# A scan step with re-paired and padded matmuls, another VectorE order, square sums on GpSimd, and the two layers written out

## The reference, cut to what matters

```
for l in range(DEPTH):
    f = swiglu(rmsnorm(x, ffn1_pre)); x = x + 0.5 * rmsnorm(f, ffn1_post)
    m, ssm, conv, pool = mixer(rmsnorm(x, mix_pre)); x = x + rmsnorm(m, mix_post)
    f = swiglu(rmsnorm(x, ffn2_pre)); x = x + 0.5 * rmsnorm(f, ffn2_post)

# the scan inside the mixer, per head, in chunks of 128 tokens
xbc = silu(conv4(xbc))                                # xs, B, C
y_intra = (C Bt * L) @ (xs * dt)                      # L: decays inside a chunk
cs = Bt @ (xs * dt * decay_to_end)                    # state that a chunk adds
state = state * chunk_decay + cs                      # chained over the chunks
y = y_intra + (C @ state_before) * exp(acum) + d_skip * xs
y = rmsnorm(y * silu(z)) @ w_ssd_branch
```

## Time and profile before

| | |
|---|---|
| timed runs (median, 3) | 2205.31 us (2205.11 to 2212.32) |
| the profiled execution, whole | 2213.59 us |
| its span, first to last instruction | 2211.8 us |
| mean granted TensorE clock | 0.964 |
| PE busy | 2081.6 us, 94% of the span |
| DVE, ACT, POOL busy | 952.4, 932.1, 1245.7 us |

### The profile page before, as it was taken

One profiled execution on the slowest core, in us unless ns is written; L12 is line 12 of the kernel. 1 busy time (PEld: TensorE's weight loads), 2 busy tenths in 40 slices (PEclk: granted clock), 3 DMA queues, 4 the chain that ended last, 5 costly groups with the idle time before them and its releaser, 6 DMA issues.

```text
span 2211.8 us, 40913 instructions
## 1 busy us (share of the span) xinstructions
PE 2081.6 (94%) x13546; PEld 2023.1 (91%) x13546; DVE 952.4 (43%) x2010; ACT 932.1 (42%) x1357; POOL 1245.7 (56%) x555
## 2 busy tenths in 40 slices
PE   6999889999999998999879998899999999989997
PEld 6999888988899997999879998889898999989997
DVE  3221177676545535221142212767665454352212
ACT  4433345555333434333334333455553334444332
POOL 5666643434356665667656666433443666656665
PEclk9999989999899999999989999999997999999998
DMA  4445423444344443444424454234433444434443
GB/s 168 142 142 158 149 74 107 128 135 140 119 141 137 142 144 103 136 143 149 143 86 142 145 155 141 80 100 138 138 127 111 156 143 140 143 96 141 142 154 109
DMA packets 86339, 292.40 MB, mean 132 GB/s; under 512 B 15728, under 2 KB 15728, under 8 KB 86256
## 3 DMA queue, kind: packets, MB, share of 16 engines
q1 hardware_dynamic: 68544, 249.13, 36.2%
q10 hardware_dynamic: 17712, 42.22, 5.5%
HBM read 269.29 MB, written 22.02 MB: 132 GB/s over the span
## 4 chain that ended last, share of the span: by engine, by line
PE 83%; DVE 8%; DVEq 3%; issue 2%; POOL 1%; ACT 1%; DMA 1%; ACTq 0%; POOLq 0%; SPq 0%
PE gb L1015 25%; PE gb L1019 23%; PE gb L1018 23%; DVEq L700 2%; PE kb L1129 2%; PE kb L1151 1%; PE kb L1137 1%; DVE gb L746 1%; POOL wlo L354 1%; PE kb L1166 1%; PE gb L1067 1%; PE kb L1160 1%; PE kb L1112 1%; PE gb L1070 1%; PE gb L1071 1%
## 5 line engine op out<-in xcount | busy, mean ns | idle before, releaser
L354 POOL TENSOR_TENSOR wlo<-wraw,whi 128x1024 fp32r<-128x1024 f32 x474 | 1139.1, 2403 | 883.3 <-ACT whi L429 864.2
L1015 PE MATMUL gb<-ahi,whi 128*128 128x336 f32 x2256 | 751.0, 333 | 23.9 <-ACT bc L496 8.2
L1019 PE MATMUL gb<-ahi,wlo 128*128 128x336 f32 x2256 | 723.0, 320 | 0.0
L1018 PE MATMUL gb<-alo,whi 128*128 128x336 f32 x2256 | 722.3, 320 | 0.0
L429 ACT ACTIVATE whi<-wraw 128x1024 fp32r<-128x1024 f32 x474 | 494.8, 1052 | 187.2 <-PE gb L1015 116.7
L1015 PEld LDWEIGHTS gb<-ahi,whi 128*128 128x128 f32 x2256 | 432.7, 192 | 38.6 <-issue 19.9
L1018 PEld LDWEIGHTS gb<-alo,whi 128*128 128x128 f32 x2256 | 433.2, 192 | 0.0
L1019 PEld LDWEIGHTS gb<-ahi,wlo 128*128 128x128 f32 x2256 | 431.0, 191 | 0.0
L1015 PE MATMUL gb<-bhi,whi 128*128 128x336 f32 x1248 | 394.7, 316 | 5.1 <-DVE blo L969 5.1
L1018 PE MATMUL gb<-blo,whi 128*128 128x336 f32 x1248 | 392.7, 315 | 0.0
L1019 PE MATMUL gb<-bhi,wlo 128*128 128x336 f32 x1248 | 392.4, 314 | 0.0
(11 more groups left out here) (166 smaller groups left out, 2177.1 us busy)
## 6 DMA issues: line engine op xcount, KB each, us to landing
wraw<-wts SPq DMA_DIRECT2D x474, 512.0 KB, 3.5
ssm_o<-tail ACTq DMA_DIRECT2D x32, 576.0 KB, 3.2
st<-ssm_in ACTq DMA_DIRECT2D x32, 512.0 KB, 3.6
x<-x_in ACTq DMA_DIRECT2D x2, 672.0 KB, 4.9
y<-x ACTq DMA_DIRECT2D x2, 672.0 KB, 3.0
pool_o<-tail ACTq DMA_DIRECT2D x2, 540.0 KB, 4.9
tail<-pst_in ACTq DMA_DIRECT2D x2, 480.0 KB, 4.2
conv_o<-cso ACTq DMA_DIRECT2D x48, 13.5 KB, 3.2
```

Of the source, the lines that this page charges most:

```text
L354: pool.tensor_tensor(wlo[:, s, :], wraw[:, s, :], whi[:, s, :].bitcast(F32), ALU.subtract).then_inc(w_lo, 1)
L1015: ins = pe.matmul(gb[bank][:, 0:T], whi[:, slot, w], xh, start=first and j == 0, stop=False)
L1018: pe.matmul(gb[bank][:, 0:T], whi[:, slot, w], xl, start=False, stop=False)
L1019: ins = pe.matmul(gb[bank][:, 0:T], wlo[:, slot, w], xh, start=False, stop=last and j == tiles - 1)
```

## The change

Five parts.

1. **Matmul shapes.** `halfr` gets 128 rows (the lower 64 zero), so L1106 contracts over 128 rows. The first chunk-state product takes all 128 rows; `bcur`'s rows outside the meta tokens are zeroed once per layer, and `group_b` becomes two copies. The intra-chunk products go chunk by chunk with the two heads side by side. The sample update becomes eight products of 32 rows, alternately on rows 0 to 31 (bank `kb2`) and 32 to 63 (bank `kb3`). The zero product is made once per layer.
2. **PE's order.** The sample update and the transposes stand ahead of the inter-chunk products; a new semaphore `yi_full` tells when the intra products are there.
3. **DVE's order.** The taps of the convolution stand between the steps of the state chain; `d_skip * xs + y_intra` is one operation right behind the chain and gives `y_read`; the states' update stands ahead of y.
4. **Square sums.** POOL adds y's squares to `acc`, with the semaphore `y_sum` for ACT, POOL itself and the mean.
5. **Layers written out.** Python loops take the place of `Fori(0, DEPTH)` on every engine, and `update_x` at the end of layer 0 interleaves the first `split_tile`s of layer 1.

```
-        halfr = sb("halfr", [HEAD_DIM, 2 * P], F32R)
+        halfr = sb("halfr", [P, 2 * P], F32R)
...
+                pool.wait_ge(sq_done, L * N_SQ + S_Y + t + 1)
+                pool.tensor_tensor(acc[:, :], acc[:, :], sq[:, 0, :], ALU.add).then_inc(y_sum, 1)
+                pool.wait_ge(y_sum, L * KI + t + 1)
...
+                act.wait_ge(y_sum, L * KI + t)
                 act.activation(sq[:, 0, :], zb, ACT.Square).then_inc(sq_done, 1)
...
-                dve.tensor_copy(bcur[:, :, :], bt[:, g, :, :]).then_inc(b_ready, 1)
+                n0 = CHUNKS[0][1]
+                dve.tensor_copy(bcur[SAMPLE:n0, 0, :], bt[SAMPLE:n0, g, 0, :])
+                dve.tensor_copy(bcur[:, 1:3, :], bt[:, g, 1:3, :]).then_inc(b_ready, 1)
...
                 if not last:
-                    conv(L, 2 * N_GROUPS + t + 1, M0["ssd"] + 2 * t + 1, XS_BANK, pair, 1 - q)
+                    conv_entry(L, nxt, M0["ssd"] + 2 * t + 1, XS_BANK, pair, 1 - q)
+                    tap(L, nxt, XS_BANK, 0)
...
                 for c, dst in ((1, pst[:, 1, :]), (2, so[:, SEQS * P:SO])):
+                    if not last:
+                        tap(L, nxt, XS_BANK, c)
...
+                dve.wait_ge(yi_full, kt + 1)
+                dve.scalar_tensor_tensor(t_a[:, 0, :], xs[:, q, :], pcol(L, G_D + t), kb[0][:, 0:T], ALU.mult, ALU.add).then_inc(y_read, 1)
+                dve.drain()
+                if not last:
+                    tap(L, nxt, XS_BANK, CONV_K - 1)
...
-            with dve.Fori(0, DEPTH) as L:
-
-                for k in range(KD):
-                    split_tile(L, k, G_F1A, 0)
+            for L in range(DEPTH):
+
+                if L == 0:
+                    for k in range(KD):
+                        split_tile(L, k, G_F1A, 0)
...
-                update_x(L, G_F2B)
+                update_x(L, G_F2B, (G_F1A, 0) if L + 1 < DEPTH else None, 1)
...
-                    ins = pe.matmul(gb[3][:, 2 * n0:2 * n0 + T], halfr[:, h * P:(h + 1) * P], rx[0:HEAD_DIM, h, :], start=h == 0, stop=h == 1)
+                    ins = pe.matmul(gb[3][:, 2 * n0:2 * n0 + T], halfr[:, h * P:(h + 1) * P], rx[:, h, :], start=h == 0, stop=h == 1)
...
-                for c, rows in ((0, slice(SAMPLE, n0)), (1, slice(0, P)), (2, slice(0, P))):
-                    ins = pe.matmul(kb[3][:, c * P:(c + 1) * P], bcur[rows, c, :], xdec[rows, c, :], start=True, stop=True)
+                for c in range(3):
+                    ins = pe.matmul(kb[3][:, c * P:(c + 1) * P], bcur[:, c, :], xdec[:, c, :], start=True, stop=True)
...
-                for h in range(2):
-                    ch = slice(h * HEAD_DIM, (h + 1) * HEAD_DIM)
-                    for c, (c0, n) in enumerate(CHUNKS):
+                for c, (c0, n) in enumerate(CHUNKS):
+                    for h in range(2):
+                        ch = slice(h * HEAD_DIM, (h + 1) * HEAD_DIM)
...
+                half = SAMPLE // 2
+                for b in range(SEQS // 2):
+                    for r in range(2):
+                        rows = slice(r * half, (r + 1) * half)
+                        ins = pe.matmul(kb[2 + r][:, b * P:(b + 1) * P], bm[rows, r * SEQS // 2 + b, :], xdec[rows, 0, :], start=True, stop=True)
+                ins.then_inc(su_full, 1)
...
-                for b in range(SEQS):
-                    ins = pe.matmul(kb[2 + b // 4][:, (b % 4) * P:(b % 4 + 1) * P], bm[:, b, :], xdec[0:SAMPLE, 0, :], start=True, stop=True)
-                ins.then_inc(su_full, 1)
```

More of the change, by code:

```diff
@@ L399, in _ @@
             pool.tensor_copy(identr[:, :], cc(C_ID))
-            pool.tensor_copy(halfr[:, :], own_in[0:HEAD_DIM, 2 * P:4 * P]).then_inc(consts, 1)
-            with pool.Fori(0, DEPTH) as L:
+            pool.tensor_copy(halfr[0:HEAD_DIM, :], own_in[0:HEAD_DIM, 2 * P:4 * P]).then_inc(consts, 1)
+            for L in range(DEPTH):
                 sum_x(L, 0, 0, 0)
@@ L551, in _ @@
             act.wait_ge(s_eps, 1)
-            with act.Fori(0, DEPTH) as L:
+            for L in range(DEPTH):
                 split_x(L, G_F1A, 0, 0, "f1i")
@@ L661, in _ @@
             dve.memset(xp[:, :], 0.0)
+            dve.memset(halfr[HEAD_DIM:P, :].bitcast(F32), 0.0)
             dve.memset(ss[:, :].bitcast(F32), 1.0)
@@ L698, in update_x @@
                     if nxt and s >= lag:
[L699 removed]
+                        split_tile(L + ahead, s - lag, *nxt)
                     dve.drain()
@@ L725, in out_tiles, with conv_entry @@
                         dve.drain()
-            def conv(L, c, m, bank, pair, side):
+            def conv_entry(L, c, m, bank, pair, side):
                 dve.wait_ge(g_full, L * N_G + m + 1)
@@ L740, in conv, with tap @@
                 dve.drain()
+            def tap(L, c, bank, k):
                 n = CW - HIST
                 cv = gb[bank][:, 0:n]
[L743 to L747, removed]
+                w = pcol(L, G_CW + CONV_K * c + k)
+                if k == 0:
+                    dve.tensor_scalar(cv, xp[:, 0:n], w, None, ALU.mult)
+                elif k < CONV_K - 1:
+                    dve.scalar_tensor_tensor(cv, xp[:, k:k + n], w, cv, ALU.mult, ALU.add)
+                else:
+                    dve.scalar_tensor_tensor(cv, xp[:, k:k + n], w, cv, ALU.mult, ALU.add).then_inc(cv_in, 1)
+            def conv(L, c, m, bank, pair, side):
+                conv_entry(L, c, m, bank, pair, side)
+                for k in range(CONV_K):
+                    tap(L, c, bank, k)
+                    if k < CONV_K - 1:
+                        dve.drain()
             def group_b(g):
-                dve.tensor_copy(bcur[:, :, :], bt[:, g, :, :]).then_inc(b_ready, 1)
+                n0 = CHUNKS[0][1]
+                dve.tensor_copy(bcur[SAMPLE:n0, 0, :], bt[SAMPLE:n0, g, 0, :])
+                dve.tensor_copy(bcur[:, 1:3, :], bt[:, g, 1:3, :]).then_inc(b_ready, 1)
             def group_b_apart(g):
@@ L911, in _ @@
                 per = TILES_PER_GROUP
+                dve.memset(bcur[:, 0, :], 0.0)
+                dve.drain()
                 group_b(0)
@@ L1161, in ssd_step @@
                 ins.then_inc(y_full, 1)
-                if first:
-                    pe.wait_ge(bm_ready, L * N_GROUPS + g + 1)
-                for b in range(SEQS):
-                    ins = pe.matmul(kb[2 + b // 4][:, (b % 4) * P:(b % 4 + 1) * P], bm[:, b, :], xdec[0:SAMPLE, 0, :], start=True, stop=True)
-                ins.then_inc(su_full, 1)
-                if not last:
-                    pe.wait_ge(y_read, kt + 1)
-                    x_token_major(L, t + 1, 1 - q)
-            with pe.Fori(0, DEPTH) as L:
+            for L in range(DEPTH):
                 ffn(L, "f1", 0, 0, 0, ST_F1A, ST_F1B)
```

44 lines of the change are left out of this document (26 added, 18 removed).

## The result

Slower, not faster: 2230.01 us (median of 4 runs, 2224.84 to 2236.53) against 2205.64, a ratio of 1.0105 with a 95% interval of 1.0072 to 1.0138. The forecast was 2156, the range ended at 2185. The profiled execution took 2230.33 us around a span of 2228.3, which is 16.5 more than the span before. The medians lie 24.4 us apart; the profiled execution of before was some 8 us above its median, so the two profiles show less of it.

A forecast was written before the change was run, and what follows sets the result against it. PE's own order of blocks was taken to bound the scan. Savings of 37.8 (regular steps), 5 (last steps) and 10.1 (layer start) made 53, less 4 for late stores: 2205.3 - 49 = 2156 us, own range 2145 to 2170, eight-in-ten 2127 to 2185.

The forecast's parts named there:

- PE's blocks: PE's work in a regular scan step: shorter blocks and a dropped wait save 1.98 us, leaving 14.2 us.
- a wait of 0.17: PE's idle time ahead of the transposes, waiting for `y_products_read`: goes, saving 0.17 us a step.
- Sample update: Sample update products in the scan step: pairs on two row groups overlap, saving 0.83 us; rival without overlap, chance 0.14.
- The loop: Scan step: DVE's chunk-state copy waits for the previous store, closing a loop that sets the step at 14.9 us.
- 10.5 + L: Step length by the store's loop: 10.5 us of work plus L, the time from store issue to landing.
- an estimate of L = 4.2 to 4.6, taken 4.4: Store's landing time in the scan: three transfers, 1.6 MB, at 415 GB/s take 3.9 us plus start and end.
- My bound from above: Rival of late stores throughout the scan: landing 5.2 us, step 15.7, time 2179 us; chance 0.08.
- The clock: Rival: PE's wait ahead of the transposes brings half clock inside the scan, 114 us lost, 2266 us; chance 0.05.
- the 0.7 us that I priced: PE's expected wait ahead of the transposes in each regular scan step, some 0.7 us.
- The last steps: Last scan step of each of the two layers, at the lower clock: 2.5 us saved each, 5 together.
- Layer start: Start of layer 1: interleaving the splits saves 10.1 us once (9 to 11); written-out layers count zero.
- square sums: Adding y's squares on POOL instead of DVE in the scan: hidden, zero effect.

The follow-up runs named there:

- e7: Changed kernel with the states' store issued as soon as the sums are ready and the next states' load directly ahead of it; 2124.32 us, ratio 0.9608.
- e10: e7 with the matmul shapes of the kernel before; 2188.81 us, ratio 0.9909.
- e2: Changed kernel with all four convolution taps ahead of VectorE's wait for the store; 2162.49 us, ratio 0.9782.
- e5: Changed kernel with the store issued ahead of the next states' load at the end of ScalarE's step; 2251.08 us, ratio 1.0183.
- e6: Changed kernel with the load of the states cut to 256 KB from the second tile on; 2195.51 us, ratio 0.9942.
- e4: Changed kernel with VectorE waiting for the store only ahead of the third piece, which writes the stored tile; 2219.39 us, ratio 1.005.
- e3: Changed kernel in its new order, but with the matmul shapes and per-step zero product of the kernel before; 2254.42 us, ratio 1.0221.
- e12: e7 with the square sums of y back on VectorE; 2125.50 us, ratio 0.9626.
- e11: e7 with the old layer start, the first half of layer 1's input split after the last update; 2131.53 us, ratio 0.9651.
- e1: Changed kernel with the store issued before ScalarE's wait for the gated value, the next states' load coming behind it; 2170.17 us, ratio 0.9831.
- e9: Kernel before with only the new matmul shapes, its VectorE order, square sums and layer start old; 2198.54 us, ratio 0.9959.

## Why the prediction was wrong

- **PE's blocks: right, and a little low.** The step of PE alone is 13.67 (e7), against my 14.2. With the old shapes in the new order it is 15.70 (e10): the shapes save 2.03, by my terms 1.81. The rest, from 16.16, is 0.46, for which I had a wait of 0.17; it came with the new order, and no run takes it apart.
- **Sample update: right.** The pairs on two row groups run beside each other: 16 records in 1.16 where 64-row ones took 2.05, a term of 0.89 for my 0.83. They start in pairs, 0.01 us between the two and 0.11 from pair to pair (e7). By the Trainium skill, "TensorEngine Tiling (Array Packing)", section "Key Properties", different tiles can load and multiply in parallel; the trace agrees. By the Trainium skill, "TensorE: Matmul & The Clock Gate", section "LDWEIGHTS (loading the stationary operand)", a 32-row load costs what a 128-row load does; the trace agrees as far as it goes, with a median of 187 ns for one of 32 rows and 188 for one of 64. Loads one behind the other would have left the 2.05; the measurement decides for overlap.
- **The loop: right in kind.** "10.5 + L" with the measured 6.6 gives 17.1; the median step is 17.0. The wait, its place, and what queues behind it are where I put them. e2 shows that part directly.
- **The step that failed is "an estimate of L = 4.2 to 4.6, taken 4.4".** I divided three transfers by the 415 GB/s of one half microsecond. With the three issued within a microsecond the rate was 217 and then 299 GB/s, and L 6.6: 2.2 us a step, 66 us over 30 steps, is about the whole distance from a gain of 38 to a loss of 28. My bound from above was 5.2, the longest landing before; but before, the store went 2.05 us behind the load and no weight load was under way in the first 4 us behind its issue, so no row showed the three together. e5 and e6 show that the load ahead makes the store late, the landings sorted behind e6 that the weight load does as much.
- **The second loop was missing.** The load of the states had landed a median of 3.6 us ahead of its use before, slack that I never read. A step shorter by 2 and a landing of 4.8 for 3.6 leave 0.4 of it; the changed kernel has 0.7 in the median, and PE waits in 15 steps. e4 and e5 show what it costs once the store's wait is out of the way.
- **The clock: a rival that I had at 0.05.** It came true, behind longer gaps than the 0.7 us that I priced: 123 us at half speed in the scans. In the changed kernel itself it adds little: from copy to copy the 11 steps with no half speed in them take 17.05 us, as the loop has it, and the 19 others 17.6, some 10 us in all. In e4 (14.5 against 20.3 in 11 steps) and e5 (15.0 against 20.5 in 13) it is most of what is lost, 64 and 71 us. That the shapes make the clock fall is ruled out from both sides: e3 has old shapes and spells, e7 new shapes and none before the scans' last steps. The gaps remain as the cause: between the second and the last transposes of the scans no run has a spell without a gap of 1.06 us or more beside it. But a gap need not bring one (below).
- **The last steps: smaller.** For 5 us together the changed kernel shows 1.0: -1.7 behind the last transposes, and in the middle stretch 9.4 saved, 0.7 less than its layer start alone. The same sums give 4.8 for e7, so the term was there once the transfers were out of the way.
- **Layer start and square sums: right in sum.** 10.07 for 10.1, and zero (e12); but that the sum came out was luck in part. I had put all of it on the interleaving and the written-out layers at zero, and in e11 6 of the 10 stay without the interleaving.

## What to carry to other kernels

A transfer that another engine waits for belongs to a loop: before an engine on the path is made shorter, read for each transfer in the step how long it had landed when it was used, and move the issue to where its data are ready, not to the end of the engine's step. A landing time holds only for the company in which it was measured; transfers that are brought together need a bound of their own. And a gap in PE can cost several times its length, so a wait of 2 us on it is to be priced with the half-speed stretch that may stand behind it.

## What the hardware showed that was not expected

- A store of 576 KB lands in some 3 us alone. With a load of 512 KB issued 0.8 us ahead on the same queue it takes 5.0, with a weight load of 512 KB from another queue beside it (and the load 1.9 us behind) 5.2 (e1), with both 6.9; with half the load (e6) the median over all steps is 5.2 in place of 6.6.
- In the scans the clock fell to 0.50 beside gaps of PE from 1.06 us (e9) to 3.2 us; the 13.6 us behind a gap of 2.07 were full of work at half speed (e1). Neither whether a spell comes nor how long it lasts follows from the gap's length: ten of e9's 30 gaps had one, 2 of the 17 gaps of 1.06 us or more in e1, and a gap of 2.46 in e5 none; gaps of 2.2 us had 3.4, 6.8 and 17.1 us.
- Products of 32 rows on two row groups start in pairs 0.01 us apart, a pair every 0.11 us, where those of 64 rows on one start 0.12 apart, (2.05 - 0.27) / 15; a load of 32 rows takes no less time than one of 64 (187 and 188 ns).
- Where the loop over layers turned, VectorE stood idle 3.34 us ahead of the next layer's first operation, with nothing that it waited for in the profile; with the layers written out that idle time is gone (e11).
